# Laying out anew the steps of three engines in a one-core transformer step with gathered experts, and splitting the last three expert ranks

## The reference, cut to what matters

```
mod = silu(c) @ w_mod + b_mod                     # shift, scale, gate, twice
h   = rmsnorm(x) * (1 + scale) + shift
q, k, v, dn_q, dn_k, dn_v, z, b, a = split(h @ w_in)
o_da = differential attention(q, k, v)            # sample tiles see cached context too
o_dn = gated DeltaNet(short_conv(dn_q, dn_k, dn_v), b, a), both directions
x   = x + gate * ([o_da, o_dn] @ w_out)
h   = rmsnorm(x) * (1 + scale) + shift
q   = (h @ w_pq) as (token, 8 heads, 2, 128);  s = q . sub_keys
top 16 of each half; the 16 x 16 sums of a head; top 16 of these
eidx, gates = 8 heads x 16 = 128 experts a token  # out of 16384
coef = gates * gelu(h . expert_u[eidx])
x   = x + gate * sum over 128 ranks of coef * expert_v[eidx]
y   = rmsnorm(x)
```

## Time and profile before

| what | value |
|---|---|
| median of 3 runs | 1320.39 us |
| the profiled execution | 1322.54 us, span 1320.7 us |
| mean granted clock of TensorE | 0.915 |
| busy: PE, DVE, POOL, ACT | 1008.7, 875.6, 561.5, 294.3 us |
| moved by DMA | 492.55 MB, 373 GB/s over the span |
| of it the gathers (queue 0) | 404.26 MB |
| of it the weights (queue 1) | 87.33 MB |

### The profile page before, as it was taken

How to read it: one execution, slowest core, us unless ns; L and a number is a source line. 1 busy time by engine, 2 the same in 40 slices (tenths; PEclk the granted TensorE clock), 3 DMA queues, 4 the chain that set the end, 5 groups by cost and what they waited for, 6 DMA issues and landing times.

```text
span 1320.7 us, 15185 instructions
## 1 busy us (share of the span) xinstructions
PE 1008.7 (76%) x5204; PEld 595.4 (45%) x5204; DVE 875.6 (66%) x2295; ACT 294.3 (22%) x755; POOL 561.5 (43%) x598
## 2 busy tenths in 40 slices
PE   7899989889899987788610386578777877776775
PEld 5757688754567774457300151233323322232322
DVE  0536349999973889523799605996779666666665
ACT  2653335323335443112100011011020000100001
POOL 0010103246676655363767677343333433333331
PEclk9899999999899998889755588789998999999999
DMA  9988368699999999999999999999999999999995
GB/s 384 365 310 320 152 223 333 234 336 413 360 409 384 332 407 358 388 366 361 368 407 409 408 408 411 385 422 422 422 420 419 420 422 422 422 421 422 422 422 208
DMA packets 96539, 492.55 MB, mean 373 GB/s; under 512 B 10704, under 2 KB 11600, under 8 KB 67920
## 3 DMA queue, kind: packets, MB, share of 16 engines
q0 software_dynamic: 83696, 404.26, 76.5%
q1 hardware_dynamic: 12768, 87.33, 16.8%
HBM read 488.93 MB, written 2.62 MB: 372 GB/s over the span
## 4 chain that ended last, share of the span: by engine, by line
PE 44%; DMA 24%; DVE 19%; issue 5%; POOL 4%; ACT 3%; SPq 0%; DVEq 0%; ACTq 0%
PE bank L1293 41%; DMA big<-in_euv,consts 16%; DVE big L2149 7%; DMA wring<-in_euv,consts 5%; POOL big L859 2%; PE bank L1299 2%; DVE extra L2149 1%; PE bank L1322 1%; DVE wring L2149 1%; DVE ops L2149 1%; DVE W L2173 1%; DMA big<-in_ev,rowT 1%; DMA extra<-in_eu,idx 1%; ACT hT L950 1%; DMA big<-in_eu,consts 1%
## 5 line engine op out<-in xcount | busy, mean ns | idle before, releaser
L1293 PE MATMUL bank<-big,W 128*32 128x512 f32 (+1 forms) x932 | 306.5, 677 | 77.9 <-DVE W L2173 56.0
L2149 DVE CUSTOM_DVE_ANT_0 big<-big,hnow 128x1024 f32<-128x1024 f32 x226 | 269.4, 1218 | 71.0 <-DMA big<-in_euv,consts 63.4
L1293 PE MATMUL bank<-wring,W 128*128 128x512 f32 (+1 forms) x456 | 172.7, 626 | 69.5 <-DVE W L2173 68.9
L1293 PEld LDWEIGHTS bank<-big,W 128*32 128x32 f32 (+1 forms) x932 | 106.4, 159 | 242.9 <-issue 238.2
L869 POOL DMA_INDIRECT big<-in_euv,consts x114 | 108.9, 955 | 152.7 <-PE bank L1293 145.1
L2149 DVE CUSTOM_DVE_ANT_0 wring<-wring,hnow 128x1024 f32<-128x1024 f32 x90 | 109.2, 1219 | 69.0 <-DMA wring<-in_euv,consts 67.0
L859 POOL DMA_INDIRECT big<-in_ev,rowT x119 | 113.2, 951 | 76.8 <-issue 36.6
L1293 PEld LDWEIGHTS bank<-wring,W 128*128 128x128 f32 (+1 forms) x456 | 63.3, 170 | 167.4 <-issue 165.9
L869 POOL DMA_INDIRECT wring<-in_euv,consts x76 | 71.8, 944 | 136.6 <-PE bank L1293 130.4
L1293 PE MATMUL bank<-big 128*128 128x128 f32 (+1 forms) x1056 | 117.1, 268 | 12.8 <-DVE big L1910 8.4
L1293 PEld LDWEIGHTS bank<-big 128*128 128x128 f32 (+1 forms) x1056 | 107.6, 181 | 28.8 <-issue 13.3
(11 more groups left out here) (360 smaller groups left out, 1479.8 us busy)
## 6 DMA issues: line engine op xcount, KB each, us to landing
wring<-in_wch SPq DMA_DIRECT2D x23, 2048.0 KB, 11.1
big<-in_wch SPq DMA_DIRECT2D x4, 1536.0 KB, 14.1
dn_tok<-in_wch SPq DMA_DIRECT2D x4, 1536.0 KB, 11.0
tok<-in_wch SPq DMA_DIRECT2D x6, 768.0 KB, 7.6
z<-in_wch SPq DMA_DIRECT2D x6, 512.0 KB, 9.5
...
```

The source lines that it names most:

```text
L1293: return nc.tensor.matmul(out, lhsT, rhs, start=first, stop=last)
L2149: V.tensor_tensor_reduce(u, u, hnow[:, :], 1.0, 0.0, ALU.mult, ALU.add, coef[t % 2][:, n:n + 1]).then_inc(dot_ready, 1)
```

## The change: three lists of steps, and the last ranks

The lists of PE, DVE and ACT are written anew up to the gathers of tile 2; in POOL's only the last line differs. The set of steps stays the same, but for the last ranks: `LAST` is 3, so the u and v rows of ranks 125 to 127 of tile 2 come apart; `SINGLES = 10`, so that the last ten ranks of tile 2 have a gelu and a spread each where eight of them were pairs (97 gelu steps become 101, and as many spread steps). On PE a new step `v_last` takes ranks 126 and 127 together: the first half of both, then the signal "half", then the second half of both. `half_sums` on ACT begins with one root of a number that is not used.

```diff
-LAST = 2
+LAST = 3
+SINGLES = 10
+LAST_LANDS = [ROWS + 8, EXTRA0, EXTRA0 + 1]
-TWOS = (... [(2, n, n + 1) for n in range(0, SLOTS - LAST, 2)] + [(2, n) for n in range(SLOTS - LAST, SLOTS)])
+TWOS = (... [(2, n, n + 1) for n in range(0, SLOTS - SINGLES, 2)] + [(2, n) for n in range(SLOTS - SINGLES, SLOTS)])
@@ half_sums (ACT)
+                nc.scalar.activation(lamv[:, 2:3], rst[:, 0:1], ACT.Sqrt)
@@ PE
+            def v_last(t):
+                ends = (SLOTS - 2, SLOTS - 1)
+                for h in range(2):
+                    for n in ends:
+                        if h == 0:
+                            pe.wait_ge(rows_in[row_slot(("gy", t, n))[0]], row_slot(("gy", t, n))[1])
+                            pe.wait_ge(*spread_ready.at(TWO_OF[t, n]))
+                        at = row(row_slot(("gx", t, n))[0])
+                        ins = mm(acc[h][:, :], spread_at(SUMS[t, n]), at[:, D + 512 * h:D + 512 * h + 512], False, n == SLOTS - 1)
+                        if h:
+                            ins.then_inc(vsum_done, 1)
+                    if h == 0:
+                        ins.then_inc(*product.next("half"))
```

The lists, at the places that the prediction speaks of (cut):

```diff
 PE, before the first gather
-x_turn.1.0 dn_s.0.1 query.0.0 query_rest.0.0 h_turn.0 key_score.0.0 query.1.0 query_rest.1.0 channels.0.1 channels.1.1
+x_turn.1.0 channels.0.1 query.0.0 query_rest.0.0 key_score.0.0 channels.1.1 query.1.0 query_rest.1.0 channels.2.1
 PE, the sample tokens and the first value batches
-qk_turn.1 dn_t.2.1.5 dn_p.2.1.6 dn_decay.1.0 token.1.1:3 token.2.1:3 token.3.1:3 dn_t.2.1.6 dn_w.2.1
+token.0.2 dn_p.2.1.2 token.1.1 dn_t.2.1.2 ... token.1.2 dn_t.2.1.4 dn_p.2.1.5 qk_turn.1 token.2.1:3 dn_decay.1.0 token.3.1:3
-v_batch.0.0.12 dn_p.1.1.2 dn_scores.2.0 dn_t.1.1.2 v_batch.0.0.13 a_turn.2.0 dn_p.1.1.3 dn_t.2.0.0 score.2.1 v_batch.0.0.14
-value.2.0 dn_t.1.1.3 score.2.2 v_batch.0.0.15
+v_batch.0.0.12:14 dn_scores.2.0 dn_t.1.1.2 score.2.1 v_batch.0.0.14:16 dn_p.1.1.3 a_turn.2.0
 PE, tile 0's second value batches
-query.0.1 query_rest.0.1 coef.0.1 v_batch.0.1.0 key_score.0.1 v_batch.0.1.1 query.1.1 query_rest.1.1 v_batch.0.1.2:5
-x_turn.1.2 query.0.2 v_batch.0.1.5 query_rest.0.2 key_score.0.2 key_score.1.1 query.1.2 v_batch.0.1.6:8 gate.1.0.0:2
-query.2.1 query_rest.2.1 query_rest.1.2 h_turn.2 key_score.1.2 v_batch.0.1.8:11 key_score.2.1 query.2.2 query_rest.2.2
-v_batch.0.1.11:15 expert_rows.1.0 v_batch.0.1.15 coef.1.0 v_batch.1.0.0:3 query.3.1 v_batch.1.0.3:5 query_rest.3.1
-v_batch.1.0.5 key_score.2.2 v_batch.1.0.6 key_score.3.1 v_batch.1.0.7 query.3.2 query_rest.3.2 v_batch.1.0.8:14
-key_score.3.2
+query.0.1 query_rest.0.1 coef.0.1 v_batch.0.1.0:2 h_turn.1 key_score.0.1 query.1.1 x_turn.1.2 query_rest.1.1 v_batch.0.1.2:4
+query.0.2 query_rest.0.2 key_score.1.1 query.1.2 query_rest.1.2 key_score.0.2 v_batch.0.1.4:6 query.2.1 v_batch.0.1.6
+query_rest.2.1 v_batch.0.1.7 key_score.2.1 v_batch.0.1.8 query.2.2 query_rest.2.2 gate.1.0.0 v_batch.0.1.9 key_score.1.2
+v_batch.0.1.10 query.3.1 v_batch.0.1.11 key_score.2.2 query_rest.3.1 v_batch.0.1.12 key_score.3.1 query.3.2 v_batch.0.1.13:16
+query_rest.3.2 gate.1.0.1 expert_rows.1.0 coef.1.0 v_batch.1.0.0:4 gate.1.1.0 v_batch.1.0.4:6 key_score.3.2
 DVE
-top_key.0.0 pair_sums.0.0.0 top_pair.0.0.0 places.0.0.0 channels.0.1 chosen.0.0.0.0:2 experts.0.0.0 channels.1.1
+channels.0.1 top_key.0.0 pair_sums.0.0.0 top_pair.0.0.0 places.0.0.0 channels.1.1 chosen.0.0.0.0:2 experts.0.0.0
-experts.1.0.0 top_key.2.1 pair_sums.1.1.0 top_pair.1.1.0 dot.1.0:4 ... dot.1.52:64 coef.1.0 top_key.3.1
-pair_sums.1.1.1 top_pair.1.1.1 places.1.1.1 chosen.1.1.1.0:2 ... chosen.1.1.0.1 experts.1.1.0 dot.1.64:67
+... top_key.2.1 pair_sums.1.1.0 top_key.2.2 top_pair.1.1.0 top_key.3.1 gate.1.0.1 slot_gates.1.0 dot.1.0:5
+dot.1.63 pair_sums.2.1.0 coef.1.0 chosen.1.1.1.1 chosen.1.1.0.1 experts.1.1.1 experts.1.1.0 top_pair.2.0.1 chosen.2.0.0.0:2
+... experts.2.1.0:2 slot_gates.1.1 dot.1.64:68 spread.1 spread.0
+dot.2.122:124 spread.95:97 dot.2.124:126 spread.97:99 dot.2.126:128 spread.100 spread.99 take.2 last_norm.2
 POOL
-gw.2.0:126 gx.2.126:128 gy.2.126:128
+gw.2.0:125 gx.2.125:128 gy.2.125:128
```

More of the change, by code:

```diff
@@ L213 @@
[L213 to L227, removed]
@@ new lines @@
+key_score.1.0 channels.4.1 h_turn.0 c_turn.1.1 channels.3.1 c_turn.0.1 channels.5.1 channels.6.1 channels.8.1
+c_turn.2.1 channels.7.1 c_turn.3.1 channels.10.1 c_turn.4.1 c_turn.5.1 query.2.0 query_rest.2.0 c_turn.6.1 c_turn.7.1
+channels.9.1 channels.11.1 c_turn.8.1 query.3.0 query_rest.3.0 c_turn.10.1 key_score.3.0 c_turn.9.1 key_score.2.0
+c_turn.11.1 mod.10 qk_turn.2 dn_decay.2.1 mod.11 dn_scores.2.1 token.0.1 mod_turn.11 dn_t.2.1.0 dn_p.2.1.1 dn_t.2.1.1
+token.0.2 dn_p.2.1.2 token.1.1 dn_t.2.1.2 dn_p.2.1.3 dn_t.2.1.3 expert_rows.0.0 dn_p.2.1.4 token.1.2 dn_t.2.1.4
@@ new lines @@
+dn_p.2.1.5 qk_turn.1 token.2.1:3 dn_decay.1.0 token.3.1:3 dn_t.2.1.5 dn_p.2.1.6 dn_scores.1.0 dn_t.2.1.6 dn_t.1.0.0
+dn_w.2.1 dn_p.1.0.1 dn_v.2.1 dn_t.1.0.1 da_turn.1 coef.0.0 v_batch.0.0.0 dn_o.2.1 da_turn.2 v_batch.0.0.1 score.1.0
+dn_p.1.0.2 v_batch.0.0.2:5 expert_rows.0.1 dn_s.2.1 dn_t.1.0.2 score.1.1 dn_p.1.0.3 v_batch.0.0.5 dn_decay.1.1
+a_turn.1.0 dn_t.1.0.3 dn_scores.1.1 score.1.2 a_turn.1.1 value.1.0 v_batch.0.0.6:8 dn_p.1.0.4 gate.0.1.0 value.1.1
+dn_t.1.0.4 score.1.3 dn_p.1.0.5 v_batch.0.0.8:10 dn_t.1.0.5 dn_p.1.0.6 a_turn.1.2 dn_t.1.0.6 dn_t.1.1.0 value.1.2
@@ new lines @@
+w_out.1.0 w_out_rest.1.0 dn_p.2.0.6 w_out.1.1 dn_t.2.0.6 w_out_rest.1.1 dn_w.2.0 dn_v.2.0 x_turn.1.1 dn_o.2.0 o_turn.2
+w_out.2.0 w_out_rest.2.0 w_out.2.1 w_out_rest.2.1 query.0.1 query_rest.0.1 coef.0.1 v_batch.0.1.0:2 h_turn.1
+key_score.0.1 query.1.1 x_turn.1.2 query_rest.1.1 v_batch.0.1.2:4 query.0.2 query_rest.0.2 key_score.1.1 query.1.2
+query_rest.1.2 key_score.0.2 v_batch.0.1.4:6 query.2.1 v_batch.0.1.6 query_rest.2.1 v_batch.0.1.7 key_score.2.1
+v_batch.0.1.8 query.2.2 query_rest.2.2 gate.1.0.0 v_batch.0.1.9 key_score.1.2 v_batch.0.1.10 query.3.1 v_batch.0.1.11
@@ L242 @@
+key_score.2.2 query_rest.3.1 v_batch.0.1.12 key_score.3.1 query.3.2 v_batch.0.1.13:16 query_rest.3.2 gate.1.0.1
+expert_rows.1.0 coef.1.0 v_batch.1.0.0:4 gate.1.1.0 v_batch.1.0.4:6 key_score.3.2 v_batch.1.0.6:16 v_slot.1.64:95
+h_turn.2 v_slot.1.95:102 gate.1.1.1 v_slot.1.102:128 v_slot.2.0:126 v_last.2
 """,
     "DVE": """
[L244 to L245 removed]
```

206 lines of the change are left out of this document (103 added, 103 removed).

## The result

The changed kernel took 1348.1 us (median of 4 runs, 1342.94 to 1351.19) against 1320.68 before: ratio 1.0217, 95% interval 1.0196 to 1.0239. It is 27 us slower; 13.5 us faster was forecast, and the range ended at 1322. The profiled execution has a span of 1346.9 us.

The account below looks back on a forecast made before the run. No engine bounds throughout; DMA is full in 650 to 730 and 870 to 1300, with transfer time unused elsewhere. Terms -3.5 - 6 + 1.5 - 2.5 - 3.0 = -13.5 us, from 1320.39, gave 1307 us; range 1294 to 1322.

Parts of the forecast that it names:

- the sentence on 870 to 1300: Wide rows, 870 to 1300: DMA engines full at 421 GB/s, only fewer bytes would help; no gain or loss counted.
- DVE's slack at the end: End of the kernel: four more gelu and spread steps of 0.2 and 0.35 us were to cost nothing.
- First gather: Up to the first gather: channels.0.1 done in DVE's idle time, -1.0 us, bounds -2.9 and +0.9.
- First gv gather and value batches of the first half: 200 to 433: token steps and value batches earlier on PE, -2.7 and -3 us; with the first gather, -3.5 arrives.
- rival B: Only the ends gain; middle gains stand still where PE's and DVE's work is the bound: 1315 us, chance 0.20.
- Rival D: Larger gain: both upstream terms arrive in full, 390 GB/s or more in 200 to 345: 1297 us, chance 0.13.
- Second value batches: Tile 0, 558 to 650: value batches between half queries shorten POOL's waits for PE, -6 us, bound -12.
- no wait over 5 us: Sign that the forecast is right: no wait of POOL over 5 us between 565 and 650.
- Tile 1's first half: 650 to 815: some 17 us of choice steps among 64 dots on DVE, +1.5 us, bounds 0 and +5.
- Rival C: Tile 1's start: dot.1.0 late behind top_key.3.1, value batches at PE's slow clock, gathers stand still: 1326 us, chance 0.14.
- Tile 1's second half: 815 to 870: earlier choice fills DVE's idle time, POOL's 15.27 us wait goes, -2.5 us, bounds -2.9 and 0.
- The end: After the last gather: halves about 2.0 us earlier, table load gone for 1.0; -3.0 us, bounds -3.7 and -0.9.

Follow-up runs that it names:

- rank order: The changed kernel with wide rows' dots, spreads and gelus back in the order of the ranks, each pair's spread right after its dots: 1309.4 us, ratio 0.9939.
- before_with_new_wide_order: The kernel before, with only the dots, spreads and gelus of tile 2's ranks 0 to 117 in the changed kernel's order: 1342.0 us, ratio 1.0180.
- before_with_new_end: The kernel before with the new end alone: three split ranks, singles for the last ten, first halves ahead, early root: 1315.89 us, ratio 0.9983.
- choice_behind_coef: The kernel in rank order, with choice steps among the dots of tile 1's first half moved behind coef.1.0: 1309.59 us, ratio 0.9944.
- five buffers: The kernel in rank order with 5 wide row buffers instead of 10: 1424.86 us, ratio 1.0821.

## Why the prediction was wrong

**The step that failed** is the sentence on 870 to 1300, "There only fewer bytes would help, and the change moves the same bytes". A full DMA share was taken for a bound that no order could break, and the new order of the wide rows' dots and spreads was given no term at all; the only steps there that the sum speaks of are the four more gelus and spreads, which "lie in DVE's slack at the end". The new order measured 37 to 39 us (changed kernel against rank order, by ratios and by medians), 35 of them behind the first wide gather. The rows could have raised the question: ten buffers at 2.49 us are 24.9 us, and the last gather before took about 16 us to land, so some 9 us seemed free for holding a buffer (some 16 to 17, as it turned out, since part of those 16 was queueing), while a list that waits for six more rows holds it 6 x 2.49 = 15 us longer.

Without that step the rest would have been right in sign: in rank order the change is 8.7 us faster (ratio 0.9939), against 13.5. By its terms, in the profile of the changed kernel; three profiles (before, before_with_new_wide_order, before_with_new_end) have the lists of before up to the wide rows and thirteen the new ones, so that each term also has a spread:

*First gather*: -1.0 forecast, +3.2 measured (203.87 against 200.67; 202.75 to 204.28 with the new lists, 200.67 to 203.18 with the old). `channels.0.1` was to run while DVE idles, but it waits there itself:

```profile
...
183.01 2.05 DVE L1751 SCALAR_TENSOR_TENSOR big<-big,params 128x256 f32<-128x256 f32 x4 [10.79 <-ACT big L975]
...
186.87 0.87 DVE L2047 MAX8 E<-xo 128x8 f32<-128x128 f32 x4 [1.81 <-ACT xo L901]
...
```

It waits for ACT until 183.01, and `top_key.0.0`, behind it in the list, starts at 186.87 instead of 182.81. The prediction asked whether DVE was idle, and not whether the operand was ready.

*First gv gather and value batches of the first half*: -2.7 and -3 forecast, and -3.5 of all three to arrive. From the first gather to the first v gather it is 141.0 us instead of 143.6: the wait of 3.04 us for the token step went as said. But the late first gather ate it up, with DVE's dots late (before, the first gather shown here was issued at 330.73) and one more wait for PE:

```profile
...
334.42 0.93 POOL L850 DMA_INDIRECT extra<-in_eu,idx  x1 [5.75 <-DVE coef L2165]
...
343.65 0.94 POOL L850 DMA_INDIRECT big<-in_eu,idx  x1 [1.85 <-PE bank L1296]
344.89 0.94 POOL L861 DMA_INDIRECT wring<-in_ev,rowT  x1 [0.30 <-issue]
...
```

The first v gather is 0.6 us later than before, the last 4.3 later (345 to 433 has 363 GB/s, not 377), so the -3 did not come: from the first to the last v gather it is 87.2 to 87.4 us with the old lists, 87.6 to 91.1 with the new. The first gather of the second batches is at 544.07, before at 544.13, and the first value batch at 557.22, before at 558.26. In this profile 1 us at most arrived: rival B's mechanism, for this part. Rival D's sign, 390 GB/s or more in 200 to 345, did not come either: it is 345.

*Second value batches*: -6 forecast. The last v gather is issued 10.4 us earlier (637.70, before 648.13); 525 to 620 has 390 GB/s instead of 373, and POOL's longest wait for PE there is 8.7 us, so "no wait over 5 us" was wrong. From the first v gather of these batches to the last it is 93.1 to 95.2 us with the new lists, 99.1 to 104.0 with the old. The term was right, on the cautious side.

*Tile 1's first half*: +1.5 forecast. Rival C did not come: POOL never waited more than 1.4 us for a dot there, and PE kept its clock (0.93 in 525 to 620). But the term was too small. DVE, with the choice steps among the dots, is busy 79.04 of 80 us in 650 to 730, the value batches begin late, and POOL waits for PE:

```profile
...
637.70 0.93 POOL L861 DMA_INDIRECT big<-in_ev,rowT  x1 [0.49 <-PE bank L1296]
...
747.07 0.94 POOL L861 DMA_INDIRECT big<-in_ev,rowT  x1 [5.80 <-PE bank L1296]
...
810.85 0.94 POOL L871 DMA_INDIRECT wring<-in_euv,consts  x1 [0.30 <-issue]
...
```

From tile 0's last v gather to the first wide gather it is 173.15 us, before 167.41 (648.13 to 815.54): 5.7 us more. With the new lists it is 171.6 to 173.2, with the old 166.1 to 167.4, so this term measured 4 to 7 us, around its upper bound of 5. With the choice steps behind the dots (choice_behind_coef) it is 169.1. All told the first wide gather comes at 803.98 to 811.11 us with the new lists and at 809.47 to 815.54 with the old, so the lead of 4.7 us in the one pair of profiles is no steady figure.

*Tile 1's second half*: -2.5 forecast. In rank order 815 to 870 runs at 422 GB/s instead of 399, 3 us, as forecast; there POOL waits 5.10 us where the 15.27 of the earlier trace rows had been. In the changed kernel the bunches begin here, and that wait is 11.11 us:

```profile
...
834.08 0.94 POOL L871 DMA_INDIRECT wring<-in_euv,consts  x1 [11.11 <-PE bank L1296]
...
```

*The end*: -3.0 forecast; alone it measured -2.2, and -3.2 from the last gather to the end of the span. The term was right. The timeline of the changed kernel has each step:

```profile
...
1333.51 0.08 DVE L2165 DVE_READ_ACCUMULATOR2_ANT coef<- 128x1 f32 x1
...
1334.99 1.28 ACT L1255 ACT_TABLE_LOAD   x1
...
1336.44 3.60 PE L1296 MATMUL bank<-wring,W 128*128 128x512 f32 x8
1338.42 0.69 DVE L2204 TENSOR_TENSOR sq<-bank,gate 128x512 f32<-128x512 f32 x1 [2.73 <-PE bank L1296]
...
1342.62 0.20 ACT L1264 ACTIVATE small<-small 128x1 f32<-128x1 f32 x1 [0.30 <-DVE small L2230]
...
```

The table load lies at 1334.99, ahead of the end, and the root at 1342.62 follows 4.2 us after DVE took the first half, before 4.9 us: 0.7 us, not 1.0. The rest, by subtraction, is the earlier half.

The Trainium skill, TensorE: Matmul & The Clock Gate, section HAM oscillation, describes short bursts between waits for data that each begin cold. The row at 991.57 agrees: four ranks in 9.38 us, where 1.8 us a rank is usual. It was not the main cause here: with the clock at 0.95 the changed list took as long.

The Trainium skill, DMA: Bandwidth & Descriptors, section Latency and other measured facts, gives about 2 us as a DMA's fixed cost. The gathers of 1 MB here took longer: the median with five buffers, when the queue was short, was 8.0 us, and the shortest single one there took 5.5; 2.5 of them are its bytes at full rate, so 5.5 and 3.0 are left. Beside other gathers the median is the figure that belongs into the cycle.

What stays open: how the 39 us divide between spreads out of rank order and bunches (about half each by one kernel), and whether more than ten buffers would give the changed list its rate back, which no run tried. Of the 5 us between the forecast and the measured gain in rank order, tile 1's first half makes most.
